# Gate rows 16 to 29 of a hybrid decoder layer: a seven-product form over token halves, read from PSUM by VectorE

## The reference

```python
xn = rms_norm(hp, norm_mix_g[l])
qa, ka, va, qr, kr, vr, gr, g_a, g_b = project_in(xn, w_in[l], pos_p)   # xn @ w_in, split
oa = diff_attn_prompt(qa, ka, va, lam)
s_p, orr = retention_prompt(qr, kr, vr, log_gamma)                       # 4 heads x 8 chunks of 128
...
a = (rms_plain(oa) * subln_g * (1.0 - lam_init)).reshape(B, T, DIFF_V_W)
r = rms_plain(orr).reshape(B, T, RET_V_W) * jax.nn.silu(gr)
m = jax.nn.sigmoid(gate_a + ba) * (a @ w_pa) + jax.nn.sigmoid(gate_b + bb) * (r @ w_pb)
hp = hp + m @ w_o
hp = hp + swiglu(rms_norm(hp, norm_ffn_g[l]), w_gu[l], w_down[l])
```

## Time and profile before

| | us |
|---|---|
| median of 3 runs | 2737.66 (2736.84 to 2738.11) |
| the profiled execution, its own time | 2737.74 |
| its span, first to last instruction | 2735.9 |
| gate stage in it, first to last of L2093 and L2069 | 997.2 to 1595.4 |

### The profile page before, as it was taken

One profiled execution on the slowest core, in us unless ns is written; L12 is line 12 of the kernel. 1 busy time (PEld: TensorE's weight loads), 2 busy tenths in 40 slices (PEclk: granted clock), 3 DMA queues, 4 the chain that ended last, 5 costly groups with the idle time before them and its releaser, 6 DMA issues.

```text
span 2735.9 us, 41660 instructions
## 1 busy us (share of the span) xinstructions
PE 2706.7 (99%) x16114; PEld 2336.4 (85%) x16114; DVE 1380.2 (50%) x2760; ACT 732.6 (27%) x1549; POOL 867.9 (32%) x697
## 2 busy tenths in 40 slices
PE   8999999999999999999999999999999999999998
PEld 6888877777777779888888899999899999998887
DVE  6431355547777764666555533243485555542224
ACT  5111122225555532232222211011332222221012
POOL 2533423302211232221122235354124444455230
PEclk9999999999999999999999999999999999999999
DMA  4323356553343234456554554334122222245221
GB/s 161 112 101 132 107 193 207 196 180 116 99 134 110 101 130 164 159 192 198 188 193 146 194 185 145 126 120 159 47 82 72 77 90 72 72 150 176 85 61 66
DMA packets 277924, 362.15 MB, mean 132 GB/s; under 512 B 28530, under 2 KB 172530, under 8 KB 277746
## 3 DMA queue, kind: packets, MB, share of 16 engines
q1 hardware_dynamic: 277746, 359.74, 39.6%
HBM read 257.24 MB, written 111.35 MB: 135 GB/s over the span
## 4 chain that ended last, share of the span: by engine, by line
PE 95%; DVE 3%; issue 1%; ACT 1%; DMA 0%; POOL 0%; SPq 0%; DVEq 0%; ACTq 0%; POOLq 0%
PE psum L538 24%; PE psum L1354 14%; PE psum L2767 14%; PE psum L2093 12%; PE psum L563 10%; PE psum L1032 3%; PE psum L1057 2%; PE psum L2749 2%; PE psum L2142 2%; PE psum L2126 1%; PE psum L2791 1%; PE psum L1468 1%; PE psum L1044 1%; PE psum L2135 1%; PE psum L1008 1%
## 5 line engine op out<-in xcount | busy, mean ns | idle before, releaser
L364 POOL TENSOR_TENSOR w_h<-stage,ones 128x512 fp32r<-128x512 f32 x268 | 307.5, 1175 | 1297.2 <-PE psum L2093 387.1
L371 POOL TENSOR_TENSOR w_l<-stage,w_h 128x512 fp32r<-128x512 f32 x268 | 357.5, 1361 | 122.4 <-DVE acc L1185 117.7
L538 PE MATMUL psum<-w_h,xt_h 128*128 128x512 f32 x864 | 343.7, 398 | 3.2 <-POOL w_l L385 2.4
L538 PE MATMUL psum<-w_h,xt_l 128*128 128x512 f32 x864 | 341.9, 396 | 0.0
L538 PE MATMUL psum<-w_l,xt_h 128*128 128x512 f32 x864 | 341.9, 396 | 0.0
L2093 PE MATMUL psum<-xt_h,w_h 128*128 128x384 f32 x744 | 264.1, 355 | 0.1
L2093 PE MATMUL psum<-xt_l,w_h 128*128 128x384 f32 x744 | 244.8, 329 | 0.0
L2093 PE MATMUL psum<-xt_h,w_l 128*128 128x384 f32 x744 | 244.7, 329 | 0.0
L416 POOL TENSOR_TENSOR w_l<-stage,w_h 128x512 fp32r<-128x512 f32 x106 | 138.7, 1309 | 269.1 <-ACT w_h L2861 269.1
L1354 PE MATMUL psum<-w_h,xt_h 128*128 128x512 f32 x512 | 219.2, 428 | 0.0
L1354 PE MATMUL psum<-w_l,xt_h 128*128 128x512 f32 x512 | 202.2, 395 | 0.0
(11 more groups left out here) (308 smaller groups left out, 5723.8 us busy)
## 6 DMA issues: line engine op xcount, KB each, us to landing
stage<-in_w_in_dram SPq DMA_DIRECT2D x88, 512.0 KB, 5.8
proj<-edge SPq DMA_DIRECT2D x112, 256.0 KB, 2.0
stage<-in_w_gu_dram SPq DMA_DIRECT2D x88, 256.0 KB, 3.8
out_dram<-acc SPq DMA_DIRECT2D x43, 512.0 KB, 3.4
acc<-proj SPq DMA_DIRECT2D x82, 256.0 KB, 3.1
gates<-edge SPq DMA_DIRECT2D x32, 544.0 KB, 3.5
acc<-in_cache_k_dram SPq DMA_DIRECT2D x32, 512.0 KB, 5.8
acc<-in_cache_v_dram SPq DMA_DIRECT2D x32, 512.0 KB, 4.6
```

Source lines behind the costliest of these rows:

```text
L364: last = nc.gpsimd.tensor_tensor(w_h[s][:, a:b, :], src, one.unsqueeze(1).to_broadcast([128, b - a, WN]), ALU.mult)
L371: last = nc.gpsimd.tensor_tensor(w_l[s][:, a:b, :], stage[h][:, a - lo:b - lo, :], w_h[s][:, a:b, :].bitcast(F), ALU.subtract)
L538: last = nc.tensor.matmul(psum[:, bank, :], x, w[s][:, k, :], start=k == 0 and n == 0, stop=k == nk - 1 and n == len(passes) - 1)
```

## The change

The 32 gate rows become 16 pairs of two rows; pair 15 and pairs 0 to 7 stay plain (three pieces a row as before). In pairs 8 to 14 (`GATE_FAST`) the first 640 tokens are taken as two halves of 320. The 256 x 1024 weights of a pair are four blocks A11, A12 (row one, k blocks 0 to 3 and 4 to 7), A21, A22, the tokens four blocks B of 512 features by 320 tokens, and the four output blocks come from seven products instead of eight: P1 = A11 B11, P2 = A12 B21, P6 = S2 T2, P7 = S3 T3, P4 = A22 T4, P5 = S1 T1, P3 = S4 B22, each 12 matmuls of 320. The last 448 tokens stay plain, in one piece a row (`PLAIN0`, `PLAIN1`, 24 matmuls of 448 each). The order of the nine units by PE's steps y = 0 to 47 of the pair: P1 0 to 3, PLAIN1 4 to 13, P2 14 to 17, PLAIN0 18 to 27, P6 28 to 31, P7 32 to 35, P4 36 to 39, P5 40 to 43, P3 44 to 47; in PLAIN1 and PLAIN0 two of ten steps hold no matmul. The two PSUM banks stay: each unit waits for the reader of the one two before it.

Readers of a pair: ACT copies P1 to SBUF and takes the sigmoids of both plain pieces; six products are read by DVE, in seven sums of 320 (`add`: P2 at y = 19, P6 at 33, P7 at 37, P4 at 41, P5 twice at 45, P3 at mark 1 of the next pair). Once the sums are made, ACT takes sigmoids in SBUF (320, 640 and 320 wide).

T1 to T4 are made once, in pairs 0 to 3: per pair DVE makes eight sums and differences of 320 at mark 5 and four low parts at mark 34, ACT four high parts at mark 20. They lie in the weight slots.

Weights: all gate weights now come pair by pair (`load_gate_pair`, two DMAs of 512 KB with runs of 1 KB, where a tile had four with runs of 2 KB). The high part of an operand is made by ACT (`gate_high`, 128 x 512), no longer by POOL; POOL makes the low parts, and in pairs 8 to 14 the sums S1 to S4: twelve instructions a pair, four in a plain one. The first pair's loads and high parts stand in the attention's steps 46 to 58. The first tile of w_pa is split likewise, by ACT and POOL, in the last pair; the second one, by POOL alone, begins after the last gate unit, and its load stands behind the stage's last waits on SP.

```diff
+GATE_PAIRS = 2 * N_FM
+GATE_SLOTS = 5
+GH, GT = 320, 640
+GATE_FAST = range(GATE_PAIRS // 2, GATE_PAIRS - 1)
+GATE_OPS = {True: ("A11", "A12", "A21", "A22"), False: ("A11", "A21", "A22", "A12", "S2", "S3", "S1", "S4")}
+GATE_SUMS = ("S3", "S2", "S1", "S4")
+GATE_STEPS = ("c11", "u2", "u3", "c21", "u4", "c22", "c12")
+P1, PLAIN1, P2, PLAIN0, P6, P7, P4, P5, P3 = range(9)
+PRODUCTS = {P1: ("A11", "B11"), P2: ("A12", "B21"), P4: ("A22", "T4"), P7: ("S3", "T3"), P6: ("S2", "T2"),
+            P5: ("S1", "T1"), P3: ("S4", "B22")}
...
+    def load_gate_pair(sp, p):
+        if p < 2:
+            sp.wait_ge(w_split, split_count(W_FM - 1, 1))
+        else:
+            sp.wait_ge(op_split, gate_op(p - 1))
+        src = w_in[0].rearrange("(k p) n -> p k n", p=128)
+        for h in range(2):
+            sp.dma_start(stage[h][:, :, 256 * (p % 2):256 * (p % 2 + 1)],
+                         src[:, 4 * h:4 * h + 4, W_FM * WN + 256 * p:W_FM * WN + 256 * (p + 1)]).then_inc(
+                             stage_loaded[p % 2], 16)
...
+        def gate_sum_made(p, name):
+            a11, a12, a21, a22 = (gate_source(p, x) for x in GATE_OPS[True])
+            if name == "S3":
+                nc.gpsimd.tensor_tensor(a21, a11, a21, ALU.subtract).then_inc(sums_ready, 1)
...
+        for p in range(GATE_PAIRS):
+            if gate_plain(p):
+                for name in GATE_OPS[True]:
+                    gate_low(p, name)
+            else:
+                for name in ("A11", "A21"):
+                    gate_low(p, name)
+                gate_sum_made(p, "S3")
+                gate_low(p, "A22")
+                gate_sum_made(p, "S2")
+                gate_low(p, "A12")
+                gate_sum_made(p, "S1")
+                gate_sum_made(p, "S4")
+                for name in ("S2", "S3", "S1", "S4"):
+                    gate_low(p, name)
...
+        for n, k in enumerate(PA_ORDER):
+            pool.wait_ge(op_high, N_GATE_OPS + n + 1)
+            last = nc.gpsimd.tensor_tensor(w_l[0][:, k, :], stage[k // 4][:, k % 4, :], w_h[0][:, k, :].bitcast(F),
+                                           ALU.subtract)
+            if n >= KD - 2:
+                last.then_inc(w_split, 1)
+        pool.wait_ge(gate_full, N_GATE_UNITS)
+        split(W_PA + 1, 1, no=tile_no(W_PA + 1), loaded=32 * (W_PA + 1))
...
+    def gate_high(act, p, name):
+        if name[0] == "S":
+            act.wait_ge(sums_ready, gate_sum(p, name))
+        else:
+            act.wait_ge(stage_loaded[p % 2], 32 * (W_FM + p // 2 + 1))
+        nc.scalar.copy(gop_h(p, name), gate_source(p, name)).then_inc(op_high, 1)
...
+    PA_ORDER = (0, 1, 2, 5, 6, 7, 3, 4)
+    PA_MARKS = {22: 0, 27: 1, 28: 2, 29: 5, 31: 6, 33: 7, 38: 3}
...
+        def wait_bank(idx):
+            if idx == 0:
+                pe.wait_ge(out_read, STEPS)
+            elif idx == 1:
+                pe.wait_ge(x_read, len(X_ORDER) - 1)
+            else:
+                if by_dve(idx - 2):
+                    p, u = gate_place(idx - 2)
+                    pe.wait_ge(v_done, gate_step(p, SUM_OF[u]))
+                else:
+                    pe.wait_ge(gate_read, gate_reads(idx - 2))
...
+        def fast_pair(p):
+            y = 0
+            for u in range(9):
+                idx = gate_unit(p, u)
+                wait_bank(idx)
+                if u in PRODUCTS:
+                    name, moving = PRODUCTS[u]
+                    pe.wait_ge(op_split, gate_op(p, name) + 1)
+                    if p == GATE_FAST[0] and moving[0] == "T":
+                        pe.wait_ge(t_step, 12)
+                    for k in range(4):
+                        sample_piece(2 * p + y // 24, y % 24)
+                        for n, (wt, low) in enumerate(((gop_h, False), (gop_h, True), (gop_l, False))):
+                            last = nc.tensor.matmul(psum[:, gate_bank(idx), 0:GH], wt(p, name)[:, k, :], gate_x(moving, k, low),
+                                                    start=k == 0 and n == 0, stop=k == 3 and n == 2)
+                        if k == 3:
+                            last.then_inc(gate_full, 1)
+                        y += 1
+                        yield
+                else:
+                    r = 0 if u == PLAIN0 else 1
+                    for k in range(KD):
+                        sample_piece(2 * p + y // 24, y % 24)
+                        wide_group(p, r, k, idx, GT, T - GT)
+                        y += 1
+                        yield
+                        if k % 4 == 3:
+                            sample_piece(2 * p + y // 24, y % 24)
+                            y += 1
+                            yield
...
+        def copy_out(p, u, dst):
+            act.wait_ge(gate_full, gate_unit(p, u) + 1)
+            nc.scalar.copy(dst, psum[:, gate_bank(gate_unit(p, u)), 0:GH]).then_inc(gate_read, 1)
+        def gated(p, name, row, a, width):
+            act.wait_ge(v_done, gate_step(p, name))
+            return nc.scalar.activation(gate_part(row, a, width), gate_part(row, a, width), ACT.Sigmoid,
+                                        bias=bias[:, row - 16:row - 15])
+        def fast_steps(p, y):
+            if y == 4:
+                if p == GATE_FAST[0]:
+                    act.wait_ge(gate_ready, 16)
+                    act.wait_ge(const_loaded, 48)
+                copy_out(p, P1, part_gb(p))
+            if y == 14:
+                wide_unit(2 * p + 1, gate_unit(p, PLAIN1), GT, T - GT, None)
+            if y == 15:
+                gate_high(act, p, "S3")
+            if y == 26:
+                gated(p, "c11", 2 * p, 0, GH)
+            if y == 28:
+                wide_unit(2 * p, gate_unit(p, PLAIN0), GT, T - GT, None)
+            if y == 29:
+                gate_high(act, p, "S1")
+            if y == 30:
+                gate_high(act, p, "S4")
+            if y == 33:
+                act.wait_ge(gate_full, gate_unit(p, P6) + 1)
+                gate_high(act, p + 1, GATE_OPS[gate_plain(p + 1)][0])
+            if y == 37:
+                act.wait_ge(gate_full, gate_unit(p, P7) + 1)
+                gate_high(act, p + 1, GATE_OPS[gate_plain(p + 1)][1])
+            if y == 41:
+                act.wait_ge(gate_full, gate_unit(p, P4) + 1)
+                gate_high(act, p + 1, GATE_OPS[gate_plain(p + 1)][2])
+            if y == 45:
+                act.wait_ge(gate_full, gate_unit(p, P5) + 1)
+                gate_high(act, p + 1, GATE_OPS[gate_plain(p + 1)][3])
...
+        def tg_sum_made(k):
+            for t, name in ((1, "B11"), (3, "B12"), (4, "B21"), (2, "B22")):
+                last = nc.vector.tensor_tensor(tg_sums(t, k), gate_x(name, k, False).bitcast(F), gate_x(name, k, True).bitcast(F),
+                                               ALU.add)
...
+        def tg_low_made(k):
+            dve.wait_ge(t_step, 3 * k + 2)
+            for t in range(1, 5):
+                last = nc.vector.tensor_tensor(tg_piece(t, k, True), tg_sums(t, k), tg_piece(t, k, False).bitcast(F), ALU.subtract)
+            last.then_inc(t_step, 1)
+        def add(p, u, dst, other):
+            dve.wait_ge(gate_full, gate_unit(p, u) + 1)
+            nc.vector.tensor_tensor(dst, psum[:, gate_bank(gate_unit(p, u)), 0:GH], other, ALU.add).then_inc(v_done, 1)
+        def fast_steps(p, y):
+            b, c = part_gb(p), part_gc
+            if y == 19:
+                dve.wait_ge(gate_read, gate_reads(gate_unit(p, P1)))
+                dve.wait_ge(gate_stored[0], 16 * (p + 1))
+                add(p, P2, gate_part(2 * p, 0, GH), b)
+            if y == 33:
+                add(p, P6, b, b)
+            if y == 37:
+                dve.wait_ge(v_done, gate_step(p, "u2"))
+                add(p, P7, c, b)
+            if y == 41:
+                dve.wait_ge(v_done, gate_step(p, "u3"))
+                dve.wait_ge(gate_stored[1], 16 * (p + 1))
+                add(p, P4, gate_part(2 * p + 1, 0, GH), c)
+            if y == 45:
+                add(p, P5, b, b)
+                add(p, P5, gate_part(2 * p + 1, GH, GH), c)
+        def last_sum(p):
+            dve.wait_ge(v_done, gate_step(p, "u4"))
+            add(p, P3, gate_part(2 * p, GH, GH), part_gb(p))
...
+                    if p in T_PAIRS and y == T_SUM_MARK:
+                        tg_sum_made(p)
+                    if p in T_PAIRS and y == T_LOW_MARK:
+                        tg_low_made(p)
+                    if y == 1 and p and not gate_plain(p - 1):
+                        last_sum(p - 1)
+                    if not gate_plain(p):
+                        fast_steps(p, y)
```

372 lines of the change are left out of this document (266 added, 106 removed).

## The result

The changed kernel takes 2753.77 us in the median (2752.50 to 2753.78, 4 runs) beside 2737.25 us of the kernel before in the same session; the ratio is 1.0059, with a 95% interval of 1.0044 to 1.0075. It is 16.5 us slower where 5.7 us faster was forecast, above the forecast's whole range of 2725 to 2744 us and above every rival. The profiled execution is one of 2753.77 us, its span 2752.0 us.

What follows compares the result with a forecast made beforehand. PE was taken as the bound: matmuls -12.8, rows 0 to 15 -4.0, T blocks +1.5, present idle in rows 16 to 31 -3.1, new waits +12.6, sum -5.8 us on 2737.7; forecast 2732 us, range 2725 to 2744.

Steps and rivals of the forecast that it cites:

- every rival: Four alternative totals for the kernel: 2727 us (chance 0.22), 2736.7 (0.22), 2745.5 and 2740 (0.16 together).
- What bounds the kernel: Whole kernel: PE, 99% busy; a change can win matmul time, win back 7 us idle, or make new waits.
- The matmuls: Pairs 8 to 14: a fast pair's matmuls save 1.8 to 1.9 us each, taken as 12.8 us in all.
- Rival (d): Pairs 8 to 14: 448 wide costs as 512, saving 0.7 us a pair, 2740 us; next to nothing, inside (c)'s 0.16.
- Pairs 8 to 14: Gate pairs 8 to 14: PE waits for DVE's late sums, POOL slowing DVE; 12.6 us, between 7.75 and 17.4.
- Rows 0 to 15: Gate rows 0 to 15: 4.0 us of PE idle won as POOL's bursts go; T blocks on DVE cost 1.5.
- Loads come 29 steps or more ahead of use: nothing: Gate stage: loads come over 20 us ahead of use, so they cost nothing.
- The merge: Merge: second w_pa tile's load and POOL's 16 instructions, about 35 us, fit under the first tile's 47.6 us; no cost.
- the clock is 0.99 to 1.00 throughout: Whole kernel: granted clock read as 0.99 to 1.00 in the profile before; no term in the sum.
- The slower rival (c): Pairs 8 to 14: DVE's longer queue delays every second chunk, 8.8 us atop 17.4 of waits, 2745.5 us; 0.16 with (d).

Runs made afterwards that it cites:

- seven moves: Three moves plus values load two steps earlier, outer products of groups 4 to 7 one step later, row 21's sample block later, T blocks before the first chunk: 2748.2 us.
- short: Kernel before with thirteen added TensorE waits ahead of the first chunk, each on one VectorE sum over 400 elements: 2751.59 us, ratio 1.0049.
- filled waits: Kernel before with three added TensorE waits on three VectorE sums over 800 elements, twelve unused matmuls issued ahead of each: 2752.1 us, ratio 1.0053.
- long ones: Kernel before with three added TensorE waits ahead of the first chunk, each on three VectorE sums over 800 elements: 2753.21 us, ratio 1.0059.
- three moves: Changed kernel with pair loads behind chunk loads, sums between root iterations (last sample block to row 30), merge's last high part ahead of two refills: 2736.2 us, ratio 0.9992.

## Why the prediction was wrong, step by step

The steps that failed are four: a wait was priced at its length, with no term for the clock and the restart (11.5 us of the 21.9 between forecast and measurement), the pair loads and POOL's relief in rows 0 to 15 (4.0), the sums' waits in pairs 8 to 14 (3.8), and the merge's first tile (2.6).

**What bounds the kernel** was right: everything that changed is PE's matmuls, PE's waits, and PE's clock.

**The matmuls** were right. In the changed kernel seven pitches of 448 take 1301.40 - 1299.97 = 1.43 us, 0.204 each:

```profile
1299.97 0.36 PE L2318 MATMUL psum<-xt_l,w_h 128*128 128x448 f32 x1
...
1301.40 0.37 PE L2318 MATMUL psum<-xt_h,w_l 128*128 128x448 f32 x1
```

Once waits, restarts and half clock (at 0.45) are taken out of the stage, all nine kernels with seven fast pairs leave -12.3 to -13.9 us against before, where -12.8 was forecast. Rival (d) is dead.

**Pairs 8 to 14** came out at 16.4 us of waits, 12.6 forecast, 7.75 to 17.4 as bounds. The places are mostly the ones named: pair 9's P3 (1.4), pair 10 (2.2, though it is the outer products that wait and not P5's bank), pair 11 (0.9), pair 13 (1.1 and 2.4, forecast 0.7), pair 14 (4.8, "longest, 3 to 6"), pair 8 (1.7). Pair 12 had none; pair 9 had two more that weren't foreseen, one of them for ACT, whose values come late by DMA. Moving the sums between the root iterations and the block by a row took 6.4 us of it: a matter of written order, as the forecast had it. The term was mis-sized by 3.8 us: in pair 14 the sample block took 4.4 us where the forecast counted 2.6, since two of its steps fell beside GpSimd's subtractions, and pair 13's P3 waited 2.4 where 0.7 was forecast.

The Trainium skill's "SBUF — State Buffer", section "SBUF: two separate sides", was weighed as what speaks against the change; the run without GpSimd's reads bears it out (0.444 to 0.281 us in the mean for one element with both inputs in SBUF, and 0.227 beside a write). It was in the sum, with the right size in the mean: 0.22 us a step above the median of 0.23 forecast, 0.22 measured (0.444). Where it falls on a single late step the mean doesn't say.

**Rows 0 to 15** failed. The forecast won back 4.0 us and paid 1.5 for the T blocks. Measured were 5.5 us of waits where 4.0 had been: before's at 1155 to 1157 and 1293 us did vanish, but 2.8 us came at 1196 us. The step that failed is "Loads come 29 steps or more ahead of use: nothing", and "nothing" again for the retention's loads behind `load_gate_pair`. It asked whether the load is early enough for its own reader and whether SP has to wait, and not how long what stands behind it takes: 1 MB in front of 256 KB that had 5.0 us (from the issue at 1184.87 to ACT's cast at 1189.84 with the loads moved). The T blocks cost what was forecast or less: their place is the 0.68 us at 1104 us, which the kernel with all pairs plain doesn't have.

The other half of that term was a misreading. The forecast had before's 4.0 us lie "during or soon after" POOL's bursts; the 1.11 us at 1096 us lie 21 us behind the end of one, and they grew to 1.59, because one of the new, spread-out subtractions now meets that `normalise`. DVE's first Newton step there, before, and then POOL and the same step after:

```profile
1093.66 0.23 DVE L2302 SCALAR_TENSOR_TENSOR psum<-o_rstd,o_var 128x1 f32<-128x1 f32 x1
```

```profile
1092.89 1.30 POOL L507 TENSOR_TENSOR w_l<-stage,w_h 128x512 fp32r<-128x512 f32 x1 [16.62 <-ACT w_h L1959]
...
1093.54 0.67 DVE L2652 SCALAR_TENSOR_TENSOR psum<-o_rstd,o_var 128x1 f32<-128x1 f32 x1
```

**The merge** failed. The forecast counted the second tile's room of 12 us, and that held. It didn't look at the first tile's last eighth, which can't be made before the last gate matmul has read its slot, and which ACT's written order puts behind two refills that wait for their loads: 2.6 us, in the kernel with all pairs plain 3.5.

**Left out altogether** were two costs of a wait, and they are the larger half of the error. The forecast said that the clock is 0.99 to 1.00 throughout and gave it no term, though before's own trace holds one fall, 3.4 us behind the 1.11 us at 1096 us. Behind waits of 1.6 to 4.8 us it fell five times, which costs 9.2 us more than before. And each wait costs 0.26 us above what its row shows, 2.3 us for nine more. Added to the misses above: 3.8 + 4.0 + 2.6 + 2.3 + 9.2 = 21.9 us, the error from -5.8 to +16.1. That it closes to the tenth is partly luck, as the 0.26 and the 0.45 are each taken from one place.

**The slower rival (c)** had its sign right and its mechanism wrong: in pairs 8 to 14 the outer products waited for a `normalise` at two places (0.90 and 2.21 us), and `update` and `inner`, whose waits it counted at every second chunk, didn't wait there at all. Its 2745.5 us is the nearest of the forecasts, which is luck.

## What to carry to other kernels

Price a new wait of TensorE as more than its length: here 0.26 us to start again, and from a length of 1 us on often 1.5 or 3.1 us of lost clock on top. Cutting a wait into pieces isn't free either, since each piece of 0.7 us pays its own 0.26. Work that another engine is given for each piece can also slow a third one where it meets it (0.23 us to 0.67 and more for a VectorE step beside a GpSimd subtraction), so look for what it meets at the tightest places and not at the mean. When a transfer is moved, ask what is behind it in its queue and how soon that is due, and when work is handed to another engine, read that engine's written order at the hand-over (here a cast behind two refills cost 2.6 us of wait). A change that saves 12.8 us on the bounding engine and lengthens its feeders' queues needs those orders redone with it; with three changes of order the loss of 16.5 us was gone, and not more than that.

## What the runs showed of the hardware

The granted clock fell to half inside or behind single waits from 1.03 us (with seven moves, at 1566 us) to 6.05 us, and stayed up behind others of 2.36, 3.19 and (with all pairs plain, in the merge) 3.54 us. The same wait of 1.8 us in the kernel before's own code, at about 1570 us, had a fall behind it in the runs with short and with filled waits and none in the run with long ones. So the same wait can cost 1.5 us more or not. The times of one kernel spread with it: 2733.6 to 2739.5 us with three moves, with mean clocks of 0.995 to 0.999, the slowest at 0.995. At half clock a matmul of 320 columns has a pitch of 0.266 us against 0.147, 1.8 times and not 2. A VectorE step of one element with two inputs in SBUF took 0.23 us beside a GpSimd write or nothing, and up to 1.36 us beside a GpSimd subtraction.
